# Squares of the next norm: eight summed on VectorE and one accumulation on TensorE in the fifth tile, instead of two in the fourth

## The chip, the cores and the metric

One core of one Trainium2 chip runs the whole kernel. The metric is the device time of one execution in microseconds; three executions were timed.

## What is computed

Four transformer layers run one after another on a sequence of 272 tokens (16 meta tokens and 256 tokens; 256 in the last two layers), width 1024, all in fp32:

```python
hs = hs + rms_norm(mix, norm_w[i, 1])                  # mix: gated delta rule (layer 0), mLSTM (layer 1)
f = conv_ffn(rms_norm(hs, norm_w[i, 2]), ...)          # up: 1024 -> 2 x 2816, conv over 3 tokens, silu, down
hs = hs + rms_norm(f, norm_w[i, 3])
...
x = layer_norm(ALPHA * x + y, ...)                     # y: convolution and attention (layer 2), GLA and MLA (layer 3)
x = layer_norm(ALPHA * x + swiglu(x, ...), ...)
```

A norm needs, for each token, the mean of 1024 squares: eight tiles of 128 channels lie on the partitions, so the sum goes over partitions and over eight tiles.

## The kernel before, in words

**Layout.** Activations lie channels by tokens: eight tiles of 128 channels, each 128 x 272 (258 or 256 columns in later phases). All weights come as one stream of 412 blocks of 128 x 1024 fp32 (`raw`, four slots), in the order of 16 phases. In a "tiles" phase a block is one output tile (8 weight squares of 128 x 128); in a "wide" phase it is one input row of all 8 outputs.

**Three products.** A block n is split: ScalarE copies it to `whi` in fp32r (`split_hi`, L411), VectorE subtracts to give `wlo` (`split_lo`, L416). TensorE then makes for each square three matmuls (`three`, L441 to L443), 24 for a tile. TensorE waits for `block_split` of a block before its tile and marks `block_used` after it. Each engine runs its instructions in the order in which the program writes them.

**Banks.** Eight PSUM banks are used in rotation, one for each output tile; `bank_free` counts how many were freed. The norm's statistic takes one bank in this rotation, ahead of the phase's tile 0, so that tile 7 of the phase takes the bank of the statistic and tile 8 that of tile 0.

**Norm put behind.** Five phases start with a norm whose scale is not ready: `up0`, `ml_in`, `up1`, `up2` and `up3`. Their matmuls take the unscaled input (`xs`), and VectorE multiplies each output tile by the scale `rs` afterwards (L948 in the up phases, L1991 in `ml_in`). `pe_tiles` runs the first three tiles together as a wave over the eight input tiles as these become ready (L462, L463, L469); tile 3 follows alone, and before its seventh square (`k == 6`) TensorE adds the statistic by two matmuls of `ones` with the sums of four squares (`fours_behind`, `sums_pe`, L683). ScalarE makes ln and exp of it (`act_scale`, L575 and L578). Then the other tiles follow, eight in a turn of a loop.

**Order on VectorE ahead of the scale** (`next_dve`, and `ln_dve` for up2 and up3): split of tile 3 (`fourth`), four sums of pairs (L745), two sums of four (L751), splits of tile 4 (`fifth`) and tile 5 (`sixth`). Behind it `ffn_dve` waits for the scale. For up0 and up1 it multiplies tiles 0 and 1 (L948), makes their convolution (four L840, each behind ScalarE's L832), multiplies tile 2, splits tile 6, multiplies tile 3, makes the convolution of tiles 2 and 3, splits tile 7, and so on: two splits, two products and four convolution steps for two tiles. For up2 and up3 the splits of tiles 6 and 7 stand behind the product of tiles 0 and 1 and one L967. In `ml_in` tile 6's split stands behind the products of the gate rows (L2005) and of tiles 1 and 2. ScalarE has the same order: `split_hi` of tile 6 is written behind the scale and the work on tiles 0 and 1.

Of the kernel before, what the change touches and what calls it, by code (L numbers as in the profile page):

```python
# [23 lines left out]
KC = D // P  # L24
N_META, SEQ = 16, 256
T1 = N_META + SEQ
T2 = SEQ
# [261 lines left out]
def build(nc, stream, params, consts, mla, last_in, hs_in, out, table):  # L289
# [128 lines left out]
    def sixth(phase):  # L418
        return FIRST_BLOCK[phase] + AHEAD + 2
# [4 lines left out]
    def fifth(phase):  # L424
        return FIRST_BLOCK[phase] + AHEAD + 1
# [19 lines left out]
    def pe_tiles(pe, phase, g0, name, count=None, meanwhile=lambda k: None, behind=None):  # L445

        b0, n = FIRST_BLOCK[phase], count or COUNT[phase]
        T = cols(phase)
        mm = nc.tensor.matmul

        if phase == "gdn_in":
            native_pe(pe, phase, g0, name)
        for k in range(KC + 1 if phase != "gdn_in" else 0):
            if k < KC:
                w = slice(k * P, (k + 1) * P)
                pe.wait_ge(*S("norm", "act").at(f"{name}_hi{k}"))
                for j in range(AHEAD):
                    o, s = rhs_out(g0 + j, phase), (b0 + j) % SLOTS
                    if k == 0:
                        pe.wait_ge(block_split, splits(b0 + j))  # L460
                        pe.wait_ge(bank_free, g0 + j + 1)
                    mm(o, whi[:, s, w], xs[:, k, T], start=(k == 0), stop=False)  # L462
                    mm(o, wlo[:, s, w], xs[:, k, T], start=False, stop=False)  # L463
            if k:
                meanwhile(k - 1)
                w = slice((k - 1) * P, k * P)
                pe.wait_ge(*S("norm", "dve").at(f"{name}_lo{k - 1}"))
                for j in range(AHEAD):
                    last = mm(rhs_out(g0 + j, phase), whi[:, (b0 + j) % SLOTS, w], xs[:, KC + k - 1, T], start=False, stop=(k == KC))  # L469
                    if k == KC:  # L470
                        last.then_inc(block_used, 1)

        def tile(j, i=0, between=None):
            g = g0 + j
            pe.wait_ge(block_split, i * 8 + splits(b0 + j))
            pe.wait_ge(bank_free, i * 8 + (g + 1))
            C = asked(j) if phase == "ml_in" else T
            for k in range(KC):
                if between and k == 6:
                    between(pe)  # L480
                last = three(bank[g % 8][:, C], (b0 + j) % SLOTS, k, xs[:, k, C], xs[:, KC + k, C], k == 0, k == KC - 1)
            last.then_inc(block_used, 1)

        head = AHEAD if phase != "gdn_in" else NATIVE
        if behind:
            tile(AHEAD, 0, behind)
            head = AHEAD + 1
        turns = (n - head) // 8
        if turns:
            with pe.Fori(0, turns) as i:  # L490
                for j in range(head, head + 8):
                    tile(j, i)
        for j in range(head + turns * 8, n):
            tile(j)
# [252 lines left out]
    def four_sum(dve, name, m, T, lo=0):  # L747
        v = S("norm", "dve")
        if m % 4 == 3:
            dve.wait_ge(*v.at(f"{name}_pair{m}"))  # L750
            nc.vector.tensor_tensor(sq[:, m, lo:T], sq[:, m - 2, lo:T], sq[:, m, lo:T], ALU.add).then_inc(*v.mark(f"{name}_four{m}"))  # L751

    def fours_in_wave(pe, name, g, T, lo=0):

        def src(m):
            return "dve", f"{name}_four{m}", sq[:, m, lo:T]

        def meanwhile(k):
            if k == 5:
                sums_pe(pe, name, src, g, ((k - 2, True, False),), T, lo)  # L760
            if k == KC - 1:
                sums_pe(pe, name, src, g, ((KC - 1, False, True),), T, lo)
        return meanwhile

    def fours_behind(name, g, T, lo=0):

        def src(m):
            return "dve", f"{name}_four{m}", sq[:, m, lo:T]

        return lambda pe: sums_pe(pe, name, src, g, ((3, True, False), (7, False, True)), T, lo)  # L770

    def next_dve(dve, post, name, row, phase):
        t = slice(PRE_FIRST[name], T1)

        def lo(m):
            dve.wait_ge(*S("norm", "act").at(f"{name}_hi{m}"))
            nc.vector.scalar_tensor_tensor(xs[:, KC + m, t], hs[:, m, t], pv("norm_w", row * KC + m), xs[:, m, t].bitcast(F32),
                                           ALU.mult, ALU.subtract).then_inc(*S("norm", "dve").mark(f"{name}_lo{m}"))

        for m in range(KC):  # L780
            add_y(dve, post, m)
            if m:
                lo(m - 1)
        lo(KC - 1)
        split_lo(dve, fourth(phase))
        for m in range(1, KC, 2):
            pair_sum(dve, name, m, T1, t.start)
        for m in range(3, KC, 4):
            four_sum(dve, name, m, T1, t.start)
        split_lo(dve, fifth(phase))  # L790
        split_lo(dve, sixth(phase))

    def next_act(act, post, name, row, g, phase):
# [1561 lines left out]
    def ln_dve(dve, n, which, layer, phase, wide, split):  # L2355
        name, g = f"ln{n}", G[f"lm{n}"]
        st, a_ = S("norm", "dve"), S("norm", "act")
        stt = nc.vector.scalar_tensor_tensor
        gain, beta = (pv(which, (2 * layer + s) * KC, KC) for s in range(2))
        total = rs[:, 1, 0:T2]  # L2360
        for m in range(KC):
            wide_done(dve, wide, m)
            stt(yt(m), X(m), ALPHA, bank[(g - 8 + m) % 8][:, 0:T2], ALU.mult, ALU.add).then_inc(*st.mark(f"{name}_y{m}"))
            if 1 <= m < YSUM:
                dve.wait_ge(*st.at(f"{name}_y{m}"))
                if m > 1:
                    dve.wait_ge(*st.at(f"{name}_ysum{m - 1}"))
                nc.vector.tensor_tensor(total, yt(0) if m == 1 else total, yt(m), ALU.add).then_inc(*st.mark(f"{name}_ysum{m}"))
            if m == 1:
                nc.vector.memset(w_bias[:, 0:1], 0.0).then_inc(bank_free, 1)  # L2370
        dve.wait_ge(*st.at(f"{name}_y{KC - 1}"))
        nc.vector.memset(w_bias[:, 0:1], 0.0).then_inc(bank_free, 7)
        if phase:
            dve.wait_ge(*a_.at(f"{name}_bhi"))
            nc.vector.tensor_tensor(xs[:, KC:2 * KC, T2:TB], alone(beta, 2), xs[:, 0:KC, T2:TB].bitcast(F32), ALU.subtract
                                    ).then_inc(*st.mark(f"{name}_blo"))
            split()

        def lo(m):
            dve.wait_ge(*a_.at(f"{name}_hi{m}"))  # L2380
            stt(xs[:, KC + m, 0:T2], yt(m), gain[:, m:m + 1], xs[:, m, 0:T2].bitcast(F32), ALU.mult, ALU.subtract
                ).then_inc(*st.mark(f"{name}_lo{m}"))

        dve.wait_ge(*S("norm", "pe").at(name + "m"))
        for m in range(KC):
            stt(yt(m), bank[g % 8][:, 0:T2], -1.0 / D, yt(m), ALU.mult, ALU.add).then_inc(*st.mark(f"{name}_c{m}"))
            if m == KC - 1:
                dve.wait_ge(*st.at(f"{name}_c{m}"))
                nc.vector.memset(w_bias[:, 0:1], 0.0).then_inc(bank_free, 1)
            if phase and m:  # L2390
                lo(m - 1)
            if phase == "od_in" and m % 2 == 0 and m:
                pair_sum(dve, name + "v", m - 1, T2)
            if phase == "od_in" and m == 5:
                four_sum(dve, name + "v", 3, T2)
        if phase:
            lo(KC - 1)
        if phase == "od_in":
            pair_sum(dve, name + "v", KC - 1, T2)
            four_sum(dve, name + "v", KC - 1, T2)  # L2400
        if phase:
            split_lo(dve, fourth(phase))
        if phase and phase != "od_in":
            for m in range(1, KC, 2):
                pair_sum(dve, name + "v", m, T2)
            for m in range(3, KC, 4):
                four_sum(dve, name + "v", m, T2)
        if phase:
            split_lo(dve, fifth(phase))
        if phase and phase != "od_in":  # L2410
            split_lo(dve, sixth(phase))

# [1074 lines left out]
    def _(pe):  # L3487
        first_pe(pe, "pre0", G["pre0"])
        pe_tiles(pe, "gdn_in", G["gdn_in"], "pre0", 32)
        gdn_pe(pe)  # L3490
        ln_behind = lambda n: fours_behind(f"ln{n}v", G[f"lv{n}"], T2)
        behind = lambda name: fours_behind(name, G[name], T1, PRE_FIRST[name])
        ln_wave = lambda n: fours_in_wave(pe, f"ln{n}v", G[f"lv{n}"], T2)
        pe_wide(pe, "gdn_out", G["gdn_out"], mix_ready("gdn"), gdn_banks_read, gdn_rows_between)
        post_pe(pe, "post0", G["post0"])
# [42 lines left out]
```

## Time and profile before

| | us |
|---|---|
| three timed executions | 1440.52, 1442.40, 1442.99 (median 1442.4) |
| the profiled execution | 1440.5 |
| its span, first to last instruction | 1438.7 |
| TensorE matmul busy in it | 1418.8 (99%) |
| VectorE busy in it | 1013.9 (70%) |
| ScalarE busy in it | 780.1 (54%) |
| mean granted TensorE clock | 0.999 of full speed |

How to read it: the span is that of the profiled execution, and its own time is 1.8 us longer than its span. A share of busy time is a mean over 16 phases. The start of a matmul is the time that orders TensorE: matmuls overlap, so that one listed as 0.29 us long starts 0.12 to 0.13 us after the one ahead.

### The profile page before, as it was taken

The numbers are of one execution on the slowest core, as the hardware profiler recorded it, in microseconds if no ns is written. First come the engines' busy times: TensorE is split into PE (matmuls) and PEld (weight loads), VectorE is DVE, ScalarE is ACT, GpSimd is POOL, SyncE is SP. The second block draws the span as 40 slices with busy tenths as digits, with TensorE's granted clock in tenths as the row PEclk, the third lists the DMA queues.
The fourth block names the chain that finished last, engine by engine and source line by source line (L and its number), as shares of the span: only waits on it lengthen the run. The fifth ranks groups of instructions, "written<-read, shape, count | busy, mean of one in ns | idle before, by whom it ended". The sixth has DMA issues, their size and how long they took to land.

```text
span 1438.7 us, 31758 instructions
## 1 busy us (share of the span) xinstructions
PE 1418.8 (99%) x11317; PEld 1359.7 (95%) x11317; DVE 1013.9 (70%) x1703; ACT 780.1 (54%) x1401; POOL 296.8 (21%) x351
## 2 busy tenths in 40 slices
PE   9999999999999999999999999999999999999997
PEld 8999888899999999999999999999999989999986
DVE  7884957659876477569897477587664687786645
ACT  6557324556655367466655356454453567654542
POOL 3804002103544000102544000013320012033310
PEclk9999999999999999999999999999999999999999
DMA  7551231244655536344656544546556433566552
GB/s 255 180 173 49 89 95 53 89 146 150 194 174 178 175 112 202 104 146 132 200 182 189 188 140 141 174 143 196 185 165 203 159 109 118 163 218 188 182 182 90
DMA packets 60997, 223.58 MB, mean 155 GB/s; under 512 B 6768, under 2 KB 6896, under 8 KB 60528
## 3 DMA queue, kind: packets, MB, share of 16 engines
q1 hardware_dynamic: 60624, 220.17, 48.1%
q10 hardware_dynamic: 288, 2.23, 0.4%
q8 instruction: 59, 0.97, 0.3%
q14 instruction: 26, 0.21, 0.0%
HBM read 221.33 MB, written 1.05 MB: 155 GB/s over the span
## 4 chain that ended last, share of the span: by engine, by line
PE 81%; DVE 12%; issue 3%; ACT 3%; DVEq 1%; ACTq 0%; POOL 0%; POOLq 0%
PE bank L441 20%; PE bank L442 20%; PE bank L443 20%; DVE wlo L416 3%; PE bank L462 2%; PE bank L1169 2%; PE bank L463 1%; PE bank L469 1%; DVE bank L948 1%; PE bank L3299 1%; PE bank L3296 1%; PE bank L3297 1%; ACT cv L832 1%; DVE cv L840 1%; DVE work L1783 1%
## 5 line engine op out<-in xcount | busy, mean ns | idle before, releaser
L416 DVE TENSOR_TENSOR wlo<-raw,whi 128x1024 fp32r<-128x1024 f32 x397 | 501.6, 1269 | 246.0 <-ACT whi L411 245.6
L441 PE MATMUL bank<-xs,whi 128*128 128x258 f32 (+2 forms) x1984 | 569.1, 287 | 0.0
L411 ACT ACTIVATE whi<-raw 128x1024 fp32r<-128x1024 f32 x397 | 415.0, 1056 | 282.6 <-PE bank L443 233.4
L442 PE MATMUL bank<-xs,whi 128*128 128x258 f32 (+2 forms) x1984 | 564.0, 284 | 0.0
L443 PE MATMUL bank<-xs,wlo 128*128 128x258 f32 (+2 forms) x1984 | 561.6, 283 | 0.0
L441 PEld LDWEIGHTS bank<-xs,whi 128*128 128x128 f32 x1984 | 374.2, 189 | 3.0 <-issue 1.6
L443 PEld LDWEIGHTS bank<-xs,wlo 128*128 128x128 f32 x1984 | 375.0, 189 | 0.0
L442 PEld LDWEIGHTS bank<-xs,whi 128*128 128x128 f32 x1984 | 374.3, 189 | 0.6 <-issue 0.2
L441 PE MATMUL bank<-hf,whi 128*128 (+3 forms) x848 | 240.9, 284 | 2.3 <-DVE cv L840 0.8
L443 PE MATMUL bank<-hf,wlo 128*128 (+3 forms) x848 | 240.4, 283 | 0.0
L442 PE MATMUL bank<-hf,whi 128*128 (+3 forms) x848 | 240.0, 283 | 0.0
L441 PEld LDWEIGHTS bank<-hf,whi 128*128 128x128 f32 x848 | 159.7, 188 | 3.8 <-issue 2.1
L442 PEld LDWEIGHTS bank<-hf,whi 128*128 128x128 f32 x848 | 159.6, 188 | 0.1
L443 PEld LDWEIGHTS bank<-hf,wlo 128*128 128x128 f32 x848 | 159.5, 188 | 0.0
L840 DVE SCALAR_TENSOR_TENSOR cv<-bank,par,cv 128x271 f32<-128x271 f32 (+4 forms) x272 | 118.5, 486 | 29.1 <-ACT cv L832 29.1
L992 POOL CAST hf<-cv 128x256 f32 (+3 forms) x88 | 57.2, 651 | 371.2 <-DVE cv L967 363.6
L832 ACT ACTIVATE cv<-bank,par 128x272 f32<-128x272 f32 (+1 forms) x120 | 64.1, 550 | 94.5 <-DVE bank L948 78.7
L994 POOL TENSOR_TENSOR hf<-cv,hf 128x256 f32 (+3 forms) x88 | 101.1, 1149 | 16.6 <-POOL hf L992 15.6
L988 POOL TENSOR_TENSOR cv<-cv 128x272 f32<-128x272 f32 (+1 forms) x44 | 46.1, 1048 | 226.1 <-ACT cv L909 226.1
L948 DVE TENSOR_TENSOR bank<-bank,rs 128x256 f32<-128x256 f32 (+2 forms) x176 | 71.1, 427 | 8.4 <-PE bank L443 6.8
L916 ACT ACTIVATE head_v<-bank 128x1 f32<-128x1 f32 x88 | 14.7, 167 | 76.9 <-DVE bank L948 76.9
L1169 PE MATMUL bank<-y,raw 128*128 128x272 f32 x208 | 50.3, 395 | 0.0
(518 smaller groups left out, 1668.9 us busy)
## 6 DMA issues: line engine op xcount, KB each, us to landing
raw<-stream SPq DMA_DIRECT2D x412, 512.0 KB, 3.7
con<-consts SPq DMA_DIRECT2D x1, 1286.5 KB, 10.4
big<-mla ACTq DMA_DIRECT2D x1, 1152.0 KB, 9.0
hs_sb<-hs SPq DMA_DIRECT2D x2, 544.0 KB, 4.2
work<-last ACTq DMA_DIRECT2D x1, 1024.0 KB, 8.4
y_out<-work SPq DMA_DIRECT2D x4, 256.0 KB, 2.1
par<-params SPq DMA_DIRECT2D x1, 420.0 KB, 7.8
par<-params SPq DMA_DIRECT2D x1, 224.0 KB, 4.8
```

Source lines behind the costliest of these rows:

```text
L411: nc.scalar.activation(whi[:, s, :], raw[:, s, :], ACT.Copy).then_inc(hi_split, 1)
L416: nc.vector.tensor_tensor(wlo[:, s, :], raw[:, s, :], whi[:, s, :].bitcast(F32), ALU.subtract).then_inc(block_split, 1)
L441: nc.tensor.matmul(out_, whi[:, slot, w], hi, start=start, stop=False)
L442: nc.tensor.matmul(out_, whi[:, slot, w], lo, start=False, stop=False)
L443: return nc.tensor.matmul(out_, wlo[:, slot, w], hi, start=False, stop=stop)
L832: nc.scalar.activation(cv[:, slot, lo:T1], bk[:, lo:T1], ACT.Identity, **args).then_inc(*steps_.mark(f"{tag}{a}"))
L840: ins = nc.vector.scalar_tensor_tensor(o[:, lo + tap:T1], bk[:, lo:T1 - tap], w[:, taps - 1 - tap:taps - tap], o[:, lo + tap:T1], ALU.mult ...
L948: nc.vector.tensor_tensor(u, u, rs[:, 0, FFN_FIRST[f]:T], ALU.mult).then_inc(*st.mark(f"u{f}_{base}_{j}{a}"))
L988: nc.gpsimd.tensor_tensor(h, cv[:, t2 % 8, t], h, ALU.mult).then_inc(*st.mark(f"h{f}_{base}_{j}"))
L992: nc.gpsimd.tensor_copy(hi, h).then_inc(*st.mark(f"hi{f}_{base}_{j}"))
L994: nc.gpsimd.tensor_tensor(lo, h, hi.bitcast(F32), ALU.subtract).then_inc(conv_taken, 2)
L1169: last = nc.tensor.matmul(o, raw[:, s, k * P:(k + 1) * P], y[:, k, :], start=(k == 0), stop=(k == KC - 1))
```

## The change

TensorE: tile 3 loses the statistic. It goes to tile 4 (the fifth), ahead of the sixth square (`k == 5`), and is one matmul of the sum of all eight squares instead of two of the sums of four. The loop of eight tiles starts a tile later. VectorE: the two sums of four are made behind the split of tile 4, not ahead of it, and one more addition makes the sum of eight, ahead of the split of tile 5. This holds for all five phases. ScalarE's order is untouched.

```diff
         def tile(j, i=0, between=None):
...
             for k in range(KC):
-                if between and k == 6:
+                if between and k == 5:
                     between(pe)
...
         if behind:
-            tile(AHEAD, 0, behind)
-            head = AHEAD + 1
+            tile(AHEAD)
+            tile(AHEAD + 1, 0, behind)
+            head = AHEAD + 2
...
+    def eight_sum(dve, name, T, lo=0):
+        v = S("norm", "dve")
+        for m in range(3, KC, 4):
+            four_sum(dve, name, m, T, lo)
+        dve.wait_ge(*v.at(f"{name}_four{KC - 1}"))
+        nc.vector.tensor_tensor(sq[:, KC - 1, lo:T], sq[:, 3, lo:T], sq[:, KC - 1, lo:T], ALU.add).then_inc(*v.mark(f"{name}_eight"))
...
-        return lambda pe: sums_pe(pe, name, src, g, ((3, True, False), (7, False, True)), T, lo)
+        return lambda pe: sums_pe(pe, name, src, g, ((KC - 1, True, True),), T, lo)
...
         for m in range(1, KC, 2):
             pair_sum(dve, name, m, T1, t.start)
-        for m in range(3, KC, 4):
-            four_sum(dve, name, m, T1, t.start)
         split_lo(dve, fifth(phase))
+        eight_sum(dve, name, T1, t.start)
         split_lo(dve, sixth(phase))
```

The same reordering stands in `ln_dve` for up2 and up3.

## Rows read from the trace of the kernel before

**Rows 1.** The page: TensorE's busy time, and its granted clock in 40 slices.

```profile
PE   1418.8 (99%) x11317; PEld 1359.7 (95%) x11317; DVE 1013.9 (70%) x1703; ACT 780.1 (54%) x1401; POOL 296.8 (21%) x351
...
PEclk9999999999999999999999999999999999999999
```

**Rows 2.** Windows: busy time in the later part of up0, of up1.

```profile
342.00:453.00 111.00, 111.00 (x889) 111.00 (x888) 93.12 (x153) 66.00 (x96) 53.87 (x58) 1.00 0.58 181
672.00:780.00 108.00, 108.00 (x906) 107.92 (x904) 96.36 (x157) 66.11 (x98) 53.61 (x60) 1.00 0.61 190
```

**Rows 3.** Timeline of TensorE in up0: tile 3, statistic, tiles 4, 6 and 7 start.

```profile
328.80 0.39 PE L441 MATMUL bank<-xs,whi 128*128 128x272 f32 x1
...
331.16 1.08 PE L683 MATMUL bank<-sq,con 128*128 128x272 f32 x4
...
332.83 0.29 PE L441 MATMUL bank<-xs,whi 128*128 128x272 f32 x1
...
338.84 0.29 PE L441 MATMUL bank<-xs,whi 128*128 128x272 f32 x1
...
341.85 0.29 PE L441 MATMUL bank<-xs,whi 128*128 128x272 f32 x1
```

**Rows 4.** Timeline of ScalarE in up0: ln of the statistic.

```profile
332.28 0.49 ACT L575 ACTIVATE rs<-bank,con_eps 128x272 f32<-128x272 f32 x1 [1.52 <-PE bank L683]
```

**Rows 5.** Timeline of VectorE in up0: sums of four, products, splits of tiles 6, 7, 9.

```profile
330.07 0.78 DVE L751 TENSOR_TENSOR sq<-sq 128x272 f32<-128x272 f32 x2
...
333.26 0.80 DVE L948 TENSOR_TENSOR bank<-bank,rs 128x272 f32<-128x272 f32 x2
...
336.47 1.22 DVE L416 TENSOR_TENSOR wlo<-raw,whi 128x1024 fp32r<-128x1024 f32 x1
...
340.29 1.21 DVE L416 TENSOR_TENSOR wlo<-raw,whi 128x1024 fp32r<-128x1024 f32 x1
...
345.81 1.22 DVE L416 TENSOR_TENSOR wlo<-raw,whi 128x1024 fp32r<-128x1024 f32 x1
```

**Rows 6.** Timelines of ml_in: tile 3, tile 4, split of tile 6, tile 6.

```profile
534.55 0.39 PE L441 MATMUL bank<-xs,whi 128*128 128x258 f32 x1
...
538.46 0.28 PE L441 MATMUL bank<-xs,whi 128*128 128x258 f32 x1
...
542.51 1.20 DVE L416 TENSOR_TENSOR wlo<-raw,whi 128x1024 fp32r<-128x1024 f32 x1
...
544.20 0.29 PE L441 MATMUL bank<-xs,whi 128*128 128x272 f32 x1
```

**Rows 7.** Timelines of up1: tile 3's wait, tile 4, split of tile 7, tile 7.

```profile
659.16 0.19 PEld L441 LDWEIGHTS bank<-xs,whi 128*128 128x128 f32 x1 [0.17 <-DVE wlo L416]
...
663.01 0.28 PE L441 MATMUL bank<-xs,whi 128*128 128x258 f32 x1
...
670.30 1.22 DVE L416 TENSOR_TENSOR wlo<-raw,whi 128x1024 fp32r<-128x1024 f32 x1
...
671.65 0.38 PE L441 MATMUL bank<-xs,whi 128*128 128x258 f32 x1
```

**Rows 8.** Timelines of up2: tile 3, tile 4, splits of tiles 6 and 7, tile 6.

```profile
947.77 0.29 PE L441 MATMUL bank<-xs,whi 128*128 128x258 f32 x1
...
951.52 0.28 PE L441 MATMUL bank<-xs,whi 128*128 128x258 f32 x1
...
954.96 2.90 DVE L416 TENSOR_TENSOR wlo<-raw,whi 128x1024 fp32r<-128x1024 f32 x2 [0.40 <-ACT whi L411]
...
957.26 0.28 PE L441 MATMUL bank<-xs,whi 128*128 128x258 f32 x1
```

**Rows 9.** Timelines of up3: split of tile 6, tile 6.

```profile
1256.65 1.23 DVE L416 TENSOR_TENSOR wlo<-raw,whi 128x1024 fp32r<-128x1024 f32 x1 [0.40 <-ACT whi L411]
...
1258.95 0.28 PE L441 MATMUL bank<-xs,whi 128*128 128x258 f32 x1
```

**Rows 10.** Timeline of TensorE's weight loads ahead of up0: a wait.

```profile
318.57 0.19 PEld L462 LDWEIGHTS bank<-xs,whi 128*128 128x128 f32 x1 [0.96 <-ACT xs L798]
```

More of the change, by code:

```diff
@@ L763, in fours_in_wave, with eight_behind @@
         return meanwhile
-    def fours_behind(name, g, T, lo=0):
+    def eight_behind(name, g, T, lo=0):
         def src(m):
-            return "dve", f"{name}_four{m}", sq[:, m, lo:T]
-        return lambda pe: sums_pe(pe, name, src, g, ((3, True, False), (7, False, True)), T, lo)
+            return "dve", f"{name}_eight", sq[:, m, lo:T]
+        return lambda pe: sums_pe(pe, name, src, g, ((KC - 1, True, True),), T, lo)
     def next_dve(dve, post, name, row, phase):
@@ L2405, in ln_dve @@
                 pair_sum(dve, name + "v", m, T2)
-            for m in range(3, KC, 4):
-                four_sum(dve, name + "v", m, T2)
         if phase:
             split_lo(dve, fifth(phase))
+        if phase and phase != "od_in":
+            eight_sum(dve, name + "v", T2)
         if phase and phase != "od_in":
@@ L3490, in _ @@
         gdn_pe(pe)
-        ln_behind = lambda n: fours_behind(f"ln{n}v", G[f"lv{n}"], T2)
-        behind = lambda name: fours_behind(name, G[name], T1, PRE_FIRST[name])
+        ln_behind = lambda n: eight_behind(f"ln{n}v", G[f"lv{n}"], T2)
+        behind = lambda name: eight_behind(name, G[name], T1, PRE_FIRST[name])
         ln_wave = lambda n: fours_in_wave(pe, f"ln{n}v", G[f"lv{n}"], T2)
```

## The prediction

> **What bounds the kernel now.** I read the page first, then windows over the stretches behind the five norms, then the timelines of TensorE, ScalarE and VectorE around each statistic. The page shows TensorE busy nearly all the span at the full granted clock [rows 1]; a kernel like this gains what TensorE is spared and loses what TensorE is made to wait. The windows show that in the later part of up0 and up1 TensorE has no idle time at all, while VectorE is busy 93.12 us of 111 and 96.36 us of 108 [rows 2]. So a wait early in such a phase is not made up later: TensorE has no gap in which to catch up, and the phase's end moves with it.
>
> What matters is then the stretch right behind a statistic. There two chains run side by side. TensorE goes on with tiles 4, 5, 6, 7; ScalarE and VectorE stand still until the statistic is there, and the split of tile 6, without which TensorE can't begin that tile, is written behind the scale on both. In up0 the statistic starts at 331.16 [rows 3], ScalarE's ln follows at 332.28, having stood idle 1.52 us for it [rows 4], the first product at 333.26, the split of tile 6 ends at 336.47 + 1.22 = 337.69 and that of tile 7 at 340.29 + 1.21 = 341.50 [rows 5]. TensorE begins tile 6 at 338.84 and tile 7 at 341.85 [rows 3]. The slack is 1.15 us at tile 6 and 0.35 us at tile 7: small against a tile of 3.0 us.
>
> **What is removed: one fp32 matmul in each of five phases.** In up0 tile 3 begins at 328.80 and tile 4 at 332.83 [rows 3]; a tile without a statistic takes 341.85 - 338.84 = 3.01. So two matmuls cost 4.03 - 3.01 = 1.02 us and one 0.51. In ml_in it is 538.46 - 534.55 = 3.91 [rows 6] less a tile of 258 columns, which takes (957.26 - 951.52) / 2 = 2.87 in up2 [rows 8]. That leaves 1.04, one matmul 0.52. Up1: 663.01 - 659.16 = 3.85 [rows 7], 0.98 and 0.49. Up2: 951.52 - 947.77 = 3.75 [rows 8], 0.88 and 0.44; up3 repeats it. TensorE is spared 0.51 + 0.52 + 0.49 + 0.44 + 0.44 = 2.4 us in all, if nothing else waits.
>
> By the Trainium skill (FP8 and Floating Point Precision, TensorE Precision Notes) true fp32 takes four passes through the array; four steps of 3.01 / 24 = 0.125 would price the matmul at 0.50, and 2.4 us for five comes out again. The trace's 0.51 agrees; I name it because a gain of this size is what the change gets if the rest of this text is wrong.
>
> **What is moved: the statistic.** It stood behind 18 matmuls of tile 3 and comes to stand behind all 24 of tile 3 and 15 of tile 4, 21 later. In up0 that is 21 x 0.125 = 2.63 us, less the 0.51 that the one matmul is shorter: the scale comes D = 2.12 us later. In the other phases 21 x 2.87/24 = 2.51, so D is 1.99 in ml_in, 2.02 in up1, 2.07 in up2 and up3. From there ScalarE's ln, exp and table load, VectorE's products and convolution, and both halves of tile 6's split follow in the same order with nothing in between that was waiting for anything else, so all of it shifts by D.
>
> **What is added on VectorE: one addition.** Two sums of four take 0.78 us [rows 5], so a third dependent one some 0.4. With the split of tile 4 (1.2) first, the sums begin near 330.07 + 1.13 = 331.2 and the eight are summed near 332.5. TensorE wants them at 328.80 + 39 x 0.125 = 333.7. Cover 1.2 us, so its price is nothing; were the cover gone, TensorE would stand inside tile 4 for the excess. The split of tile 4 ends near 331.3 and is wanted at 331.8; the split of tile 5 ends near 333.7 and is wanted at 335.3. VectorE's next work is the first product, now 333.26 + 2.12 = 335.4, so the fourth sum is hidden too. No DMA is issued from the moved code. The raw slot of tile 4's block is given back a little earlier and that of tile 5's about 0.4 us later, with more than two tiles left until they are read. The loop on TensorE begins a tile later and leaves seven tiles of up to 44 as plain code. Its price is unknown from both sides: nothing, as tile starts inside and outside the loop stand the same 3.01 apart, up to a few tenths for each phase. I take nothing.
>
> **The sum, phase by phase.** After the change TensorE begins tile 6 or 7 when its split has ended, plus the hand-over: up1's tile 7 was already in that state, since its split ended at 670.30 + 1.22 = 671.52 and it began at 671.65, a matmul of 0.38 where the others are 0.28 to 0.29 [rows 7]. I take 0.1 for the hand-over.
>
> - up0, tile 7: 341.50 + 2.12 + 0.1 = 343.7, against 341.85 before: +1.9. (Tile 6: 337.69 + 2.22 = 339.9 against 338.84, +1.1, so it waits too; tile 7 decides.)
> - ml_in, tile 6: 542.51 + 1.20 + 1.99 + 0.1 = 545.8 against 544.20 [rows 6]: +1.6.
> - up1, tile 7: slack nothing, so all of D: +2.0.
> - up2, tile 6: the first of two splits begins at 954.96 [rows 8]; with 1.22 for one, 956.18 + 2.07 + 0.1 = 958.35 against 957.26: +1.1.
> - up3, tile 6: 1256.65 + 1.23 + 2.17 = 1260.05 against 1258.95 [rows 9]: +1.1.
>
> These hold the 2.4 us that are spared: TensorE comes to the split 0.5 us sooner and waits 0.5 longer. Sum 7.7 us. It doesn't grow in the later tiles: VectorE does two tiles of up0 in 345.81 - 340.29 = 5.52 us [rows 5] against TensorE's 6.02, so from tile 8 on it runs ahead again. Against the profiled execution's own 1440.5 (span 1438.7 and 1.8 around it) that makes 1448.2. The median of the three runs is 1442.4, 1.9 above the profiled one, so my number for a median is 1442.4 + 7.7 = 1450.1. A change of 0.2% is 2.9 us, about what a measurement of this kernel can tell from no change.
>
> **The rivals.**
>
> *Hidden by the banks, faster.* The tiles rotate through eight banks and tile 0's is not asked for before tile 8, so a later scale only makes VectorE run further behind, and TensorE keeps its 2.4 us. Place: the start of tile 8, 341.85 + 3.01 = 344.86, against the end of tile 0's convolution before 336.47 [rows 5]: 8 us of slack. It would decide if tile 6's split were not written behind the scale, or if D stayed under 1.15 us in up0. Time 1442.4 - 2.4 = 1440.0. Chance 0.05. The Trainium skill (Perfetto Trace Analysis, Optimizing Tensor Performance, Matmuls) says that independent matmul groups should rotate through the banks so that the next group's matmuls cover the reading out of the last. By that rule alone the move would be free and the time this 1440.0. The bank slack agrees with it here; the weight splits are a second resource that it doesn't count.
>
> *No slack anywhere, slower still.* Each phase passes on all of D, as up1 does: 2.12 + 1.99 + 2.02 + 2.07 + 2.07 = 10.3, or 1452.7. For it: VectorE's row in up0 is full, and its waits for ScalarE could grow as the two fall out of step with GpSimd. Against: the slacks of 1.15 and 0.35 us above. Chance 0.08.
>
> *Half absorbed.* ScalarE or VectorE has idle time behind the scale that shrinks (it stood 1.52 us idle ahead of the ln [rows 4], but that is ahead of it), or TensorE makes some up in the waits at a phase's end. Then about half of 7.7, 1446.3. Chance 0.08.
>
> *The clock.* A wait of over 1 us could cost TensorE its clock. Before up0 it waited 0.96 us [rows 10] and the granted clock stays at 9 in every slice [rows 1], the 2.4 GHz level; the new waits are up to 1.5 us. If one tile ran at half the clock it would cost 3.0 us more, in all five 15 us. Chance 0.02. The Trainium skill (TensorE: Matmul & The Clock Gate, HAM oscillation) warns that idle gaps between groups of matmuls bring the clock down; no slice here shows that.
>
> **How the numbers follow.** The forecast has 0.77, with its own range 1448.3 to 1451.8: 0.3 either way for each phase's D and hand-over, and what three runs differ. The rivals hold 0.05, 0.08, 0.08 and 0.02. Leaving out the fast end and the clock, the range is 1446.0 to 1452.9. Slower by over 0.2% (above 1445.3) are the forecast, full D, the clock and nearly all of the half: 0.92. The bank rival's 1440.0 is inside 0.2% (1439.5 to 1445.3), and some of the half: 0.06. Faster 0.02.
>
> **What the changed profile would show.** The statistic as two rows of L683 pieces instead of four, about 5.0 us behind the start of tile 3. ScalarE's ln idle ahead of it 3.6 us in up0 instead of 1.52. TensorE's weight load with an idle time of 1 to 1.5 us at tile 6 and under 1 at tile 7 in up0, released by VectorE's L416; one such wait in ml_in, up2 and up3. The time from tile 3's start to tile 8's start longer by 1.9 in up0, 2.0 in up1. Wrong would be: no wait on L416 behind the statistic (the banks' rival), a wait on the L751 sum inside tile 4 (the added addition is on the path), or a VectorE that keeps TensorE waiting past tile 9.

## The result, and the profile after

The changed kernel is slower. Five executions had a median of 1450.57 us (1449.57 to 1451.61), five of the kernel before 1442.4 us; the ratio is 1.0063, with a 95% interval of 1.0052 to 1.0073. Later comparisons timed the kernel before 15 to 27 times beside each set of experiments and gave medians of 1440.5 to 1440.7, and there the changed kernel stood at 1.0064 (1.0050 to 1.0078). Some executions of either kernel are 2 to 3 us longer than others and show a lower mean granted clock, so a median shifts with how many of them it holds; the last section has what was seen of that.

The page of the changed kernel, first line and part 1:

```profile
span 1448.8 us, 31703 instructions
...
PE 1419.7 (98%) x11307; PEld 1359.6 (94%) x11307; DVE 1017.3 (70%) x1708; ACT 779.5 (54%) x1401; POOL 296.4 (20%) x351
```

The span is 10.1 us longer, TensorE's busy time 0.9 us: the rest is idle time of an engine that had almost none. The view of waits of TensorE names it in one line (who waited for whom, us in total, times, the longest):

```profile
PE bank L441 <- DVE wlo L416: 9.0, 8, 1.9
```

Eight waits for a weight split, 9.0 us; seven of them, 8.9 us, stand in the five phases, and one of 0.2 us, at 277.63, ahead of all that the change touches. Before, the same line of this view held 0.2 us. The timeline of TensorE in up0 answers to [rows 3]; the brackets are the idle time ahead and what ended it:

```profile
328.77 0.39 PE L441 MATMUL bank<-xs,whi 128*128 128x272 f32 x1
...
333.76 0.62 PE L684 MATMUL bank<-sq,con 128*128 128x272 f32 x2
...
339.95 0.39 PE L441 MATMUL bank<-xs,whi 128*128 128x272 f32 x1 [1.44 <-DVE wlo L416]
...
343.77 0.39 PE L441 MATMUL bank<-xs,whi 128*128 128x272 f32 x1 [0.56 <-DVE wlo L416]
...
346.88 0.29 PE L441 MATMUL bank<-xs,whi 128*128 128x272 f32 x1
```

These are tile 3, the statistic (two pieces instead of four, 4.99 us behind tile 3 instead of 2.36), and tiles 6, 7 and 8. From tile 3 to tile 7 it is 15.00 us, against 13.05 before. The timelines of ScalarE and of VectorE in the same stretch answer to [rows 4, 5]:

```profile
334.42 0.49 ACT L576 ACTIVATE rs<-bank,con_eps 128x272 f32<-128x272 f32 x1 [3.69 <-PE bank L684]
```

```profile
332.00 0.44 DVE L759 TENSOR_TENSOR sq<-sq 128x272 f32<-128x272 f32 x1
...
335.40 0.80 DVE L955 TENSOR_TENSOR bank<-bank,rs 128x272 f32<-128x272 f32 x2 [1.83 <-ACT rs L579]
...
338.61 1.21 DVE L416 TENSOR_TENSOR wlo<-raw,whi 128x1024 fp32r<-128x1024 f32 x1
...
342.43 1.22 DVE L416 TENSOR_TENSOR wlo<-raw,whi 128x1024 fp32r<-128x1024 f32 x1
```

ScalarE sits idle 3.69 us for the statistic instead of 1.52. VectorE has the added addition (332.00) done 1.3 us before TensorE wants it, and then sits idle 1.83 us for the scale. The splits of tiles 6 and 7 end at 339.82 and 343.65, and TensorE begins each tile 0.12 to 0.13 us behind. The other four phases show the same at tile 6, up1 also at tile 7:

```profile
547.79 0.39 PE L441 MATMUL bank<-xs,whi 128*128 128x272 f32 x1 [1.94 <-DVE wlo L416]
...
552.43 0.29 PE L441 MATMUL bank<-xs,whi 128*128 128x272 f32 x1
...
675.22 0.38 PE L441 MATMUL bank<-xs,whi 128*128 128x258 f32 x1 [1.52 <-DVE wlo L416]
...
678.95 0.38 PE L441 MATMUL bank<-xs,whi 128*128 128x258 f32 x1 [0.60 <-DVE wlo L416]
...
965.96 0.38 PE L441 MATMUL bank<-xs,whi 128*128 128x258 f32 x1 [1.41 <-DVE wlo L416]
...
1268.89 0.38 PE L441 MATMUL bank<-xs,whi 128*128 128x258 f32 x1 [1.41 <-DVE wlo L416]
```

The second row is tile 7 of ml_in, 4.64 us behind tile 6, where a tile of 272 columns takes 3.01. The windows (the third figure from the end is the granted clock) show why:

```profile
549.00:550.00 1.00, 1.00 (x6) 1.00 (x5) 0.76 (x1) 0.99 (x2) 0.00 (x0) 0.50 0.77 279
550.00:551.00 1.00, 1.00 (x6) 1.00 (x6) 0.00 (x0) 0.94 (x3) 0.00 (x0) 0.50 0.59 238
...
552.00:553.00 1.00, 1.00 (x10) 1.00 (x9) 1.00 (x2) 1.00 (x2) 0.00 (x0) 1.00 0.48 180
```

TensorE is busy all the time, but 6 matmuls fall into a window of one microsecond instead of 10 (matmuls that overlap its edges are counted with it). The granted clock is 0.50 of full speed there, the 1.2 GHz level.

For all kernels below I measured each phase in the same way: the distance from the start of tile 3 to the start of tile 11, when all waits behind the statistic are over, less the same distance before (25.07, 24.56, 24.06, 23.82 and 23.83 us). It can't see what happens outside these stretches, and it is free of differences between executions elsewhere.

| | up0 | ml_in | up1 | up2 | up3 | sum | median, us | ratio to before (95%) |
|---|---|---|---|---|---|---|---|---|
| changed | 2.06 | 3.23 | 2.06 | 1.24 | 1.30 | 9.9 | 1450.57 | 1.0063 (1.0052 to 1.0073) |
| changed, again | 2.06 | 1.71 | 2.08 | 1.24 | 1.29 | 8.4 | 1451.57 | 1.0064 (1.0050 to 1.0078) |
| 1 position alone | 2.75 | 4.09 | 2.80 | 1.66 | 1.72 | 13.0 | 1454.11 | 1.0079 (1.0062 to 1.0096) |
| 2 one matmul, fourth tile | 0.15 | -0.08 | 0.32 | -0.41 | -0.42 | -0.4 | 1440.49 | 0.9993 (0.9983 to 1.0002) |
| 3 three squares sooner | 0.94 | 0.82 | 1.08 | 0.27 | 0.33 | 3.4 | 1444.34 | 1.0021 (1.0011 to 1.0030) |
| 4 split ahead | -0.18 | 1.44 | 0.03 | -0.44 | 0.32 | 1.2 | 1442.55 | 1.0006 (0.9996 to 1.0015) |
| 5 filled wait | 2.04 | 1.70 | 2.06 | 1.24 | 1.30 | 8.3 | 1450.97 | 1.0071 (1.0056 to 1.0087) |
| 6 ml_in alone | 0.00 | 1.69 | 0.00 | 0.00 | 0.00 | 1.7 | 1442.70 | 1.0019 (1.0009 to 1.0029) |
| 7 before, split ahead | 0.00 | -0.02 | -0.14 | 0.00 | -0.01 | -0.2 | 1440.13 | 0.9997 (0.9988 to 1.0006) |
| 8 sooner and split ahead | -0.43 | 0.56 | -0.47 | -0.32 | -0.34 | -1.0 | 1439.46 | 0.9993 (0.9984 to 1.0002) |
| 9 as 8, up phases alone | -0.43 | 0.00 | -0.47 | -0.33 | -0.33 | -1.6 | 1438.48 | 0.9987 (0.9978 to 0.9996) |

Medians of experiments stand beside a before of 1440.5 to 1440.7.

The totals expected for runs 1 to 4 were reckoned from the 1442.4 of the first comparison, while the kernel before took 1440.62 beside them. So their misses are read from the differences in rows and not from the totals: run 2 hits its 1440.5 and run 3 comes within 0.3 us of its 1444.6 only because of that shift.

### The profile page after: what moved, and what is told of

Its sections match the earlier page's. It is cut to its first block, busy times and chain, and to the rows that moved or that the text cites. A ratio compares the mean times of both kernels' runs of the same rounds, so it can differ in the third digit from the quotient of the medians.

```text
span 1448.8 us, 31703 instructions
## 1 busy us (share of the span) xinstructions
PE 1419.7 (98%) x11307; PEld 1359.6 (94%) x11307; DVE 1017.3 (70%) x1708; ACT 779.5 (54%) x1401; POOL 296.4 (20%) x351
## 4 chain that ended last, share of the span: by engine, by line
PE 79%; DVE 12%; ACT 4%; issue 4%; DVEq 1%; ACTq 0%; POOL 0%; POOLq 0%
PE bank L441 20%; PE bank L442 20%; PE bank L443 19%; DVE wlo L416 4%; PE bank L462 2%; PE bank L1176 2%; PE bank L463 1%; DVE bank L955 1%; PE bank L469 1%; PE bank L3306 1%; PE bank L3303 1%; PE bank L3304 1%; ACT cv L839 1%; DVE cv L847 1%; DVE work L1790 1%
## 5 line engine op out<-in xcount | busy, mean ns | idle before, releaser
L416 DVE TENSOR_TENSOR wlo<-raw,whi 128x1024 fp32r<-128x1024 f32 x397 | 502.9, 1271 | 244.6 <-ACT whi L411 244.1
```

What stands on the lines that cost most here:

```text
L416: nc.vector.tensor_tensor(wlo[:, s, :], raw[:, s, :], whi[:, s, :].bitcast(F32), ALU.subtract).then_inc(block_split, 1)
```

## The experiments

**1. The position alone.** On the kernel before:

```diff
-                if between and k == 6:
+                if between and k == 5:
...
-            tile(AHEAD, 0, behind)
-            head = AHEAD + 1
+            tile(AHEAD)
+            tile(AHEAD + 1, 0, behind)
+            head = AHEAD + 2
```

> The statistic alone is moved to tile 4, ahead of the sixth square, as two matmuls of the sums of four; VectorE keeps its order of before. Theory of the late splits: the scale comes 21 matmuls later and nothing is spared, D = 2.63 us in up0 and 2.51 elsewhere; less the slack of the split that decides (0.25, 0.39, 0, 0.98, 0.97 us) this gives 2.4 + 2.1 + 2.5 + 1.5 + 1.5 = 10.0 us over before in rows, and 1.6 us more for each tile in which the clock falls, so 1452 to 1456. Theory that VectorE's added sum or its new order costs the time: the order is that of before, so not over 3 us above before. Theory that the plain code of seven tiles behind the loop costs it: the code is there, 8 us above before, but with no wait for a split of tile 6.

It came out at 1454.11 us, 13.0 us over before in rows where 10.0 were expected. ml_in had a tile at half the clock again, which is some 1.5 of the 3.0. Most of the rest is in up0, ml_in and up1: the splits of tile 4 came just too late there as well (tile 3 took 3.25 us in up0, where the changed kernel takes 3.11), a wait that the two matmuls of the statistic inside tile 3 had hidden. The place costs all of the change's loss and more; VectorE's new order and the single matmul give some of it back. VectorE's addition as the cause is out. So is the plain code of the seven tiles behind the loop: the time here is spent in waits for L416 (8.9 us of them in the view of waits), and run 4, which has the same code, is 1.2 us over before.

**2. The arithmetic alone.** On the kernel before:

```diff
-                if between and k == 6:
+                if between and k == 7:
...
         for m in range(3, KC, 4):
             four_sum(dve, name, m, T1, t.start)
+        eight_of_fours(dve, name, T1, t.start)
         split_lo(dve, fifth(phase))
...
-        return lambda pe: sums_pe(pe, name, src, g, ((3, True, False), (7, False, True)), T, lo)
+        return lambda pe: sums_pe(pe, name, src, g, ((KC - 1, True, True),), T, lo)
```

> The arithmetic alone: VectorE adds all eight, right behind the sums of four and ahead of the split of tile 4; TensorE makes one matmul, but in the fourth tile (tile 3), ahead of its eighth square; the loop is that of before. Theory of the late splits: the scale comes 3 matmuls later and 0.5 us is spared, so D is -0.1 us; up0 -0.4, ml_in -0.5, up1 -0.1, up2 and up3 -0.4 each: 1.9 us under before, 1440.5. Theory that the added sum costs the time: it stands on VectorE here too, ahead of two splits, so over before by several us.

1440.49 us beside 1440.62: no change that can be told, 0.4 us less in rows instead of 1.9. Up2 and up3 gained the 0.4 expected of each; up0, ml_in and up1 did not gain. The timeline of VectorE in up0, with TensorE's tile 4 behind it, shows where the 0.5 us went:

```profile
330.99 0.44 DVE L756 TENSOR_TENSOR sq<-sq 128x272 f32<-128x272 f32 x1
331.35 2.35 DVE L416 TENSOR_TENSOR wlo<-raw,whi 128x1024 fp32r<-128x1024 f32 x2
```

```profile
332.70 0.39 PE L441 MATMUL bank<-xs,whi 128*128 128x272 f32 x1
```

The first of the two splits ends at 331.35 + 1.22 = 332.57 and TensorE begins tile 4 behind it, 0.3 us later than its matmuls would allow. In up1 tile 7's split is late too. The addition is free only where a slack covers it. In this place it is on the path, a part of what the matmul gave.

**3. Three squares sooner.** On the changed kernel `k == 5` becomes `k == 2`.

> The changed kernel, with its one matmul three squares (9 matmuls) sooner, ahead of the third square of tile 4. Theory of the late splits: D is 1.1 us less than in the changed kernel in each phase, 0.9 to 1.0; up0 +0.7, ml_in +0.5, up1 +0.9, up2 and up3 0.0: 2.2 us over before, no tile at the lower clock, 1444.6. If the sum of eight isn't ready then, TensorE waits inside tile 4 by up to 0.1. Theory that it doesn't depend on the place (added sum, code): as the changed kernel, 1450.6.

1444.34 us, in rows 3.4 us over before where 2.2 were expected. From the start of tile 3 to ScalarE's ln it took 1.10, 0.87, 0.97, 0.97 and 0.97 us less in the five phases than in the changed kernel, and the rows fell by 1.1, 0.9, 1.0, 1.0 and 1.0 us (ml_in without its slow tile). The time follows the delay one for one, as it must where a late split decides. Up2 and up3 kept 0.3 where I expected nothing: the ln came 1.11 us later than before (4.34 us behind tile 3, against 3.23), not 0.9 to 1.0, and the first matmuls behind a wait start 0.1 us later than in a running row.

**4. The split of tile 6 ahead of the scale.** On the changed kernel; the statistic stays late. The edit for ScalarE is the same as that for VectorE:

```diff
         eight_sum(dve, name, T1, t.start)
         split_lo(dve, sixth(phase))
+        split_lo(dve, sixth(phase) + 1)
```

Its later place is taken out: the first pair's split in up2 and up3, that of tile 2 in ml_in, and in up0 and up1 tile 7's split moves to it, for which `pairs` makes the pair of tiles 2 and 3 ahead of a loop of four turns.

> The changed kernel with the statistic where it is, as late as it is, but the split of tile 6 written ahead of the scale on ScalarE and VectorE in all five phases; in up0 and up1 tile 7's split takes the place that tile 6's had (for this the pair of tiles 2 and 3 stands ahead of the loop). Theory of the late splits: the waits at tiles 6 and 7 go and TensorE keeps most of the 2.4 us, with perhaps 0.7 us of wait left at tile 8 of ml_in: -0.5, +0.2, -0.5, -0.4, -0.4, 1440.8, and no tile at the lower clock. Theory that the late scale costs by the banks or by the products: the scale is as late as before, so 1448 to 1451.

The scale is as late as in the changed kernel (in up0 the ln is 5.64 us behind tile 3, against 5.65), and the rows are 1.2 us over before instead of 9.9, or instead of 8.4 if the slow tile is left out: 1442.55 us. So 7.2 us of the loss hang on the place of the splits that the edit moves, tile 6's and in up0 and up1 tile 7's as well. This is the run that speaks against the banks and the products as the cause. It isn't the 1.6 us under before that was expected. TensorE has 2.4 us less to do and still comes out 1.2 us later, so some 3.6 us of waiting are left, and what is left is for splits of later tiles, which still stand behind the scale: 0.37 us at tile 9 of up1, 0.25 at tile 8 of up3 and, the largest, 0.94 us at tile 7 and 0.40 at tile 8 of ml_in. In ml_in the splits of tiles 7 to 9 stand behind the gates' chain on ScalarE, which begins with the scale. The timeline of VectorE in ml_in:

```profile
543.70 0.43 DVE L2031 TENSOR_TENSOR work<-work,rs 4x272 f32<-4x272 f32 x1 [2.69 <-ACT work L1995]
...
547.07 1.23 DVE L416 TENSOR_TENSOR wlo<-raw,whi 128x1024 fp32r<-128x1024 f32 x1 [1.59 <-ACT whi L411]
```

Tile 7's split waits 1.59 us for its upper half, which ScalarE makes behind four operations on the gate rows.

**5. A filled wait in ml_in.** On the changed kernel:

```diff
         def tile(j, i=0, between=None):
             g = g0 + j
+            if phase == "ml_in" and j == 6:
+                pe.wait_ge(bank_free, g + 1)
+                for _ in range(FILL):
+                    nc.tensor.matmul(bank[g % 8][:, 0:T2], xs[:, 0, 0:P], xs[:, 1, 0:T2], start=True, stop=True)
```

> The changed kernel; in ml_in alone TensorE makes 8 more fp32r matmuls of 256 columns on the norm's input ahead of tile 6, into tile 6's own bank, which its first matmul then overwrites. In the changed kernel it waits there 1.94 us and the granted clock then falls to 0.50 for about 3 us, which makes tile 6 4.64 us long instead of 3.01. Theory that the length of the idle time brought the clock down: the 8 take 0.9 us of the wait, tile 6 begins when it did, the clock stays and ml_in is +1.6 over before instead of +3.2, so 1.6 us under the changed kernel (1449.0). Theory that the fall is chance, or is set by what ml_in does otherwise: tile 6 stays 4.6 us long, 1450.6, or the fall comes and goes from run to run.

In its profile tile 6 began when it did (11.26 us behind tile 3), the wait was 0.99 us and the clock stayed at 1.00. But the median of its four executions was 1450.97, not 1449.0, though the profiled one took 1449.31. Inconclusive: in the next run the clock stayed without any filling.

**6. ml_in alone changed,** the four up phases as before: the conditions of the diff hold for `phase == "ml_in"` only.

> The change in ml_in alone; the four up phases as before. Theory of the late splits, with the clock's fall behind the long wait: +3.2 in rows of ml_in and nothing elsewhere, 1443.8. Without a fall of the clock: +1.6, 1442.2. Theory that the phases hang together (a delay in one is given back in the next): under +1.

1442.70 us, 1.7 us more in rows, and nothing given back in later phases. Windows behind the same wait of 1.94 us:

```profile
545.81 0.39 PE L441 MATMUL bank<-xs,whi 128*128 128x272 f32 x1 [1.94 <-DVE wlo L416]
```

```profile
546.00:548.00 2.00, 2.00 (x17) 2.00 (x17) 1.31 (x2) 1.97 (x3) 0.00 (x0) 1.00 0.51 137
548.00:550.00 2.00, 2.00 (x18) 2.00 (x17) 0.76 (x3) 1.94 (x4) 0.00 (x0) 1.00 0.80 240
```

The clock is 1.00 throughout. The same idle time brought it down in one profile and not in another.

**7. The kernel before with the split ahead,** the same edit as in run 4.

> The kernel before, with the split of tile 6 ahead of the scale as in the run on the changed kernel, and the statistic in its old place. Theory of the late splits: the splits were not late here but for a slack of nothing in up1, so 0 to -0.2: 1440.6. Theory that moving the splits is a gain of its own, which would have hidden what the late scale costs in the other run: 1438.5 or less. Theory that it costs (products 1.2 us later on VectorE): 1442 or more, mostly in ml_in.

1440.13 us beside 1440.69, inside the interval of no change, -0.2 us in rows. Moving the split is no gain of its own, so run 4 took away the loss itself.

**8. Sooner, and the split ahead:** the edits of runs 3 and 4 together.

> The changed kernel with the statistic three squares sooner and the split of tile 6 ahead of the scale. Theory of the late splits: the waits left at tiles 7 to 9 go with 1.1 us less delay; TensorE is spared 0.4 in up0, 0.3 in ml_in, and 0.3 to 0.4 in each of the others, less than one matmul since tile 4 begins 0.1 late behind its split: 1.7 us under before, 1438.9. Rival: waits of the size left in the other run (0.94 and 0.40 in ml_in) hang on the gates' chain and not on the scale, so 1440.6 or more.

1439.46 us. The four up phases gained as expected, 0.3 to 0.5 us each. In ml_in neither theory holds whole: the 0.94 at tile 7 went, as the theory of the late splits had it, and the 0.40 at tile 8 stayed, as the rival had it, so that ml_in lost 0.56.

**9. The same in the four up phases alone,** ml_in as before.

> The version with the statistic three squares sooner and the split of tile 6 ahead of the scale, but in the four up phases alone; ml_in as before. In the rows of the run with all five, the up phases stood 0.43, 0.47, 0.32 and 0.34 us under before and ml_in 0.56 over it. Theory of the late splits: 1.6 us under before in rows, 1439.1, and the only one of these versions with an interval under 1. Rival: the gain of the up phases is lost in what follows them, 1440.6.

1438.48 us beside 1440.53, ratio 0.9987 with an interval that ends at 0.9996: the one version whose interval lies below 1. In rows it is 1.6 us, near the 1.9 that one fp32 matmul in each of four phases is worth.

**10. The changed kernel again.**

> The changed kernel once more, for the clock and for its distance to before with many executions. In its profile the granted clock fell behind the wait of 1.94 us in ml_in, but with ml_in alone changed the same wait came without a fall. If the fall is chance, this profile may show it, or not, and another stretch may; rows without a fall are 8.4 us over before (2.1, 1.7, 2.1, 1.2, 1.3), 1.6 more with one in ml_in. If the fall belongs to the changed kernel, tile 6 of ml_in is again 4.6 us long and the median is 10 us over before.

1451.57 us. Tile 6 of ml_in waited 1.94 us again, at full clock, and the five phases were 8.4 us over before. Another stretch had the low clock in this profile, ahead of all that the change touches:

```profile
120.00:124.00 4.00, 4.00 (x19) 3.64 (x20) 1.69 (x5) 1.14 (x5) 0.00 (x0) 0.50 0.00 0
```

It put tile 3 of up0 at 331.20 instead of 328.77. Two of the five executions, 1448.98 and 1449.11 us, had the full mean clock of 0.999; the other three, 1451.57 to 1452.06, had 0.997. The eight executions of the kernel before beside them with 0.999 lie from 1440.25 to 1440.68, around 1440.42. At like clock the distance is 8.6 us, against 8.4 in rows.

## Why the prediction was right

The time forecast was 1450.1, the measured 1450.57, and it came by the mechanism forecast. That the two totals are only 0.5 us apart is partly luck, as the last paragraph of this section shows. Step by step:

**The bound.** "A wait early in such a phase is not made up later" held: from tile 9 to tile 11 the tile starts are as far apart as before again (3.01 us in up0, 2.87 in up1), and with ml_in alone changed (run 6) the later phases have the lengths of before, 0.00 in the table.

**The delay of the scale.** D was forecast as 2.12 us in up0. From tile 3 to ScalarE's ln it took 5.65 us, against 3.48 before [rows 3, 4]: 2.17. In the other four phases it was 2.03, 2.07, 2.08 and 2.08, against 1.99 to 2.07 forecast.

**The decision at tile 6 or 7.** Forecast +1.9, +1.6, +2.0, +1.1, +1.1, in all 7.7 us. Rows without a slow tile (run 10) give 2.1, 1.7, 2.1, 1.2, 1.3, in all 8.4. Each is 0.1 to 0.2 short, which fits a D that was longer by 0.01 to 0.05 us and the hand-over: I priced it at 0.1, it is 0.12 to 0.13, and the first matmuls behind a wait start 0.1 later than in a running row. The waits stood where they were named: up0 1.44 and 0.56 us at tiles 6 and 7, ml_in, up2 and up3 at tile 6. In up1 I named tile 7 alone; tile 6 waited 1.52 us first and tile 7 decided, as in up0. The new waits were put at up to 1.5 us, but the prediction's own terms give more in ml_in: the 1.6 us by which tile 6 is late and the 0.5 that TensorE is spared ahead of it, 2.1. Measured were 1.94.

**The matmul spared** is real: runs 8 and 9 keep it in the up phases, 0.3 to 0.5 us in each, near the 0.44 to 0.51 of the sum.

**The added addition** was priced at nothing with a cover of 1.2 us; in the changed kernel it was ready 1.3 us ahead. Run 2 gives its price where the cover is gone: about 0.3 us in up0.

**The rivals.** *Hidden by the banks* fell: the bank of tile 0 never decided. In run 4, with tile 6's split out of the way, none of TensorE's waits at tiles 7 to 9 is for a bank either; those that the trace gives a releaser are for splits. *Half absorbed* fell too: nothing was given back, neither behind the waits nor at a phase's end, for the span grew by 10.1 us, the 9.9 in rows and 0.2 more. *No slack anywhere* (10.3 us) was not far for up0 and up1, too much for the other three. *The clock*, at 0.02, was taken too lightly: one tile of ml_in ran at half the clock in the profile of the changed kernel and made it 4.64 us long, where the same tile behind the same wait took 3.11 in run 10: 1.5 us, half of the 3.0 that the rival gave a tile, because the clock was low for only part of it. The profile's 9.9 us in rows are 8.4 and this.

**How near the total came.** The 7.7 us forecast are the terms of the phases, each 0.1 to 0.2 short; at like clock the step is 8.6 us (run 10), of which 8.4 stand in the five stretches and 0.2 to 0.3 outside them, which no run traces to a place. The base was 1442.4, the median of three executions from 1440.52 to 1442.99, where the kernel before takes 1440.4 at full clock. That and the measured step make 1449.0, where the two executions of run 10 at full clock stand. The five executions behind the 1450.57 had mean clocks of 0.997 and 0.998; in the profiled one, 1450.62, the slow tile of ml_in is 1.5 us of it. So a base 2.0 us high made up for a step forecast 0.9 us short and for most of what the clock cost. By the prediction's own other number, 1448.2 from the profiled execution at full clock, the miss is 0.9 us.

## What to carry to other kernels

Before a result is moved later, list everything that is written behind it on the engines that wait for it, also what doesn't need it: here the scale was in no hurry, but the next weight split stood behind it in program order, and TensorE needs that split within two tiles. With the split moved ahead first, the statistic three squares sooner and ml_in left as it was (run 9), the single matmul gained 1.6 us in rows where the changed kernel lost 8.4. A slack is a row minus a row; the 0.35 us at tile 7 of up0 could be read from the kernel before, and the time followed the delay one for one once such slacks were used up (run 3).

## What was not expected of the hardware

The granted clock falls in some executions and not in others behind the same idle time. A wait of 1.94 us in ml_in was followed by about 3 us at half clock in two profiles (the changed kernel and run 1) and by none in two others (runs 6 and 10). Runs 1, 3 and 10 had the clock at 0.50 from 120 to 124 us (in run 10 from 119 to 125), in a stage that none of the edits touches. The last wait of TensorE ahead of it was one of 0.57 us at 117.00 in run 10; the kernel before has the same wait, 0.56 us at 116.75, and kept its clock. Tile 3 of up0 then began at 331.2 to 331.5 us instead of 328.8; run 4 had a shorter one (0.57 in those 4 us, tile 3 at 329.48); the profile of the kernel before had no such stretch. Executions of the kernel before lie from 1440.3 to 1444.0 us, a spread of the size of such a fall, and their mean granted clocks go with it: of the 25 beside runs 1 to 4, the 14 from 1440.26 to 1440.63 us had 0.999, the four from 1442.22 to 1442.43 had 0.998 and the seven from 1442.70 to 1444.02 had 0.996 or 0.997. So the longer ones did run with a lower clock somewhere. Where in them it fell is open, as none of them was profiled.
